# GpSimd builds every other second one-hot of the first tile, ScalarE the first ones of those quads

## The reference

```python
scores = einsum('thpc,hpnc->thpn', q, sub_keys)          # 8 heads, 2 halves, 128 keys
vals, idx = top_k(scores, 16)
top_vals, top_c = top_k(cand, 16)                        # of 16 x 16 sums per head
experts = (i1 * 128 + i2).reshape(T, 128)                # 128 of 16384 experts per token
gates = softmax(top_vals).reshape(T, 128)
# per block of 128 tokens:
u = take(expert_down, experts)                           # rows of 2048
hdn = gelu(einsum('ted,td->te', u, x))
y = einsum('te,ted->td', gates * hdn, take(expert_up, experts))
h = h + y;  return rms_norm(h, final_norm_gain)
```

## Time and profile before

| | |
|---|---|
| median of three runs | 2942.48 us |
| profiled execution | 2936.86 us |
| its span | 2935.1 us |
| PE busy | 2811.8 us (96%) |
| DVE busy | 2050.6 us (70%) |
| ACT busy | 1118.3 us (38%) |
| POOL busy | 542.0 us (18%) |
| row operations, down (L1976) | 256, 345.6 us, mean 1352 ns |
| gathers of down rows (L735) | 256, 261.6 us, mean 1022 ns |
| gathers of up rows (L735) | 256, 270.4 us, mean 1056 ns |

### The profile page before, as it was taken

How to read it: one execution, slowest core, us unless ns; L and a number is a source line. 1 busy time by engine, 2 the same in 40 slices (tenths; PEclk the granted TensorE clock), 3 DMA queues, 4 the chain that set the end, 5 groups by cost and what they waited for, 6 DMA issues and landing times.

```text
span 2935.1 us, 40591 instructions
## 1 busy us (share of the span) xinstructions
PE 2811.8 (96%) x15985; PEld 2275.7 (78%) x15985; DVE 2050.6 (70%) x3115; ACT 1118.3 (38%) x1743; POOL 542.0 (18%) x534
## 2 busy tenths in 40 slices
PE   6999999999999999899999999999999989999997
PEld 4788888887879988798897799888888877444443
DVE  4688877778765456744655669985559999666666
ACT  3344444445454445644455542112027986000000
POOL 1000000000000000000000002334435457544443
PEclk9999999999999999999999999999999999999999
DMA  9988888887866635365443646999998888999997
GB/s 362 361 288 271 270 269 269 270 268 269 294 201 179 174 112 167 124 201 170 136 130 122 202 135 231 351 339 409 407 356 284 295 295 322 408 409 409 409 409 319
DMA packets 345757, 799.55 MB, mean 272 GB/s; under 512 B 40104, under 2 KB 95648, under 8 KB 344800
## 3 DMA queue, kind: packets, MB, share of 16 engines
q1 hardware_dynamic: 270576, 505.70, 50.6%
q0 software_dynamic: 74992, 291.27, 26.4%
HBM read 794.76 MB, written 2.10 MB: 271 GB/s over the span
## 4 chain that ended last, share of the span: by engine, by line
PE 67%; DMA 14%; DVE 6%; ACT 5%; issue 4%; POOL 4%; SPq 0%; DVEq 0%; ACTq 0%; POOLq 0%
PE ps L2042 16%; PE ps L2044 15%; PE ps L2043 15%; PE ps L2607 13%; DMA s<-in_up_rows,s 12%; POOL s L735 3%; DVE s L1995 2%; DVE r L1268 1%; ACT s L1185 1%; DMA s<-in_down_rows,s 1%; DMA s<-in_ret_first 1%; DVE s L1976 1%; ACT s L1155 1%; ACT s L1163 1%; PE ps L2342 1%
## 5 line engine op out<-in xcount | busy, mean ns | idle before, releaser
L2042 PE MATMUL ps<-r,r 128*128 128x256 f32 (+1 forms) x2976 | 999.9, 336 | 14.8 <-DVE r L1268 12.4
L2044 PE MATMUL ps<-r,r 128*128 128x256 f32 (+1 forms) x2976 | 980.1, 329 | 0.0
L2043 PE MATMUL ps<-r,r 128*128 128x256 f32 (+1 forms) x2976 | 979.3, 329 | 0.0
L1268 DVE TENSOR_TENSOR r<-s,r 128x1024 fp32r<-128x1024 f32 (+2 forms) x532 | 640.1, 1212 | 418.9 <-ACT r L750 417.0
L750 ACT CAST r<-s 128x1024 fp32r<-128x1024 f32 (+2 forms) x532 | 549.0, 1039 | 740.2 <-PE ps L2044 696.8
L2042 PEld LDWEIGHTS ps<-r,r 128*128 128x128 f32 x2976 | 569.0, 191 | 81.0 <-issue 21.2
L2043 PEld LDWEIGHTS ps<-r,r 128*128 128x128 f32 x2976 | 569.3, 191 | 52.6 <-issue 5.3
L2044 PEld LDWEIGHTS ps<-r,r 128*128 128x128 f32 x2976 | 568.3, 191 | 50.5
L2732 PE MATMUL ps<-s,big 128*128 128x512 f32 x1024 | 441.6, 594 | 1.5 <-DMA s<-in_up_blocks 1.5
L1995 DVE SCALAR_TENSOR_TENSOR s<-s,s,s 128x1024 f32<-128x1024 f32 x256 | 328.8, 1284 | 162.3 <-DMA s<-in_up_rows,s 160.6
L1976 DVE CUSTOM_DVE_ANT_0 s<-s,s 128x1152 f32<-128x1152 f32 x256 | 345.6, 1352 | 97.3 <-DMA s<-in_down_rows,s 97.1
(11 more groups left out here) (315 smaller groups left out, 2244.1 us busy)
## 6 DMA issues: line engine op xcount, KB each, us to landing
s<-in_ada_w SPq DMA_DIRECT2D x128, 512.0 KB, 5.5
s<-in_up_blocks SPq DMA_DIRECT2D x128, 512.0 KB
s<-in_ret_w_in SPq DMA_DIRECT2D x112, 512.0 KB, 5.3
s<-in_down_blocks SPq DMA_DIRECT2D x128, 448.0 KB
s<-in_w_in SPq DMA_DIRECT2D x96, 512.0 KB, 3.9
s<-in_ret_w_out SPq DMA_DIRECT2D x64, 512.0 KB, 5.8
s<-in_ret_w_in SPq DMA_DIRECT2D x112, 256.0 KB, 4.1
s<-in_mla_w_in SPq DMA_DIRECT2D x48, 512.0 KB, 3.9
```

The costliest lines, as they stand in the source:

```text
L1268: v.tensor_tensor(lo_of(w), raw_of(w), hi_of(w).bitcast(F), ALU.subtract).then_inc(*lo_made.to(w))
L2042: pe.matmul(o, lh, rh, start=start, stop=False, skip_group_check=True)
L2043: pe.matmul(o, lh, rl, start=False, stop=False, skip_group_check=True)
L2044: return pe.matmul(o, ll, rh, start=False, stop=stop, skip_group_check=True)
```

## The change

`by_pool(t, q)` is true for the odd quads of tile 0. For them GpSimd makes the second ones, times the coefficients, into a buffer of its own, OHG, of four `tensor_scalar` instructions of 128x128: is LESS (minus i) equal to SECOND (minus i2), times CFT, the coefficient. ScalarE makes the first ones without coefficient, out of the PSUM bank: one Abs and one Relu of 128x512, into OH1[0]. VectorE has nothing to do in these quads. The even quads stay as they were.

```diff
+        OHG = at(W + 6144, 4, 128)
+        def by_pool(t, q):
+            return t == 0 and q % 2 == 1
...
+        ONES_AT = {min(195 + 2 * q, 255): q for q in range(1, 32, 2)}
...
+                if b == 129:
+                    sp.wait_ge(*built.at((0, 31)))
...
+            def pool_ones(q):
+                if q == 1:
+                    g.wait_ge(*block_used.at(127))
+                    g.wait_ge(*coef_copied.at(0))
+                else:
+                    g.wait_ge(*built.at((0, q - 2)))
+                for k in range(4):
+                    c = 4 * q + k
+                    r = g.tensor_scalar(OHG[:, k, :], LESS.bitcast(F), SECOND[0][:, c:c + 1], CFT[0][:, c:c + 1],
+                                        ALU.is_equal, ALU.mult)
+                r.then_inc(*pool_hot.to((0, q)))
...
+                if n in ONES_AT:
+                    pool_ones(ONES_AT[n])
...
-                    for k in range(4):
-                        c = 4 * q + k
-                        r = s.activation(o2[:, k, :], STEP, ACT.Abs, bias=SECOND[0][:, c:c + 1])
+                    if by_pool(0, q):
+                        o2 = OH1[0]
+                        s.wait_ge(*compared.at((0, q)))
+                        r = s.activation(flat(o2), bank[0], ACT.Abs)
+                    else:
+                        for k in range(4):
+                            c = 4 * q + k
+                            r = s.activation(o2[:, k, :], STEP, ACT.Abs, bias=SECOND[0][:, c:c + 1])
...
-                if n in HOT_AT:
+                if n in HOT_AT and not by_pool(0, HOT_AT.index(n)):
                     first_ones(0, HOT_AT.index(n))
...
-                free[b] = first_hot.at((t, q))
+                free[b] = (less_read if by_pool(t, q) else first_hot).at((t, q))
...
-                pe.wait_ge(*first_hot.at((t, q)))
+                pe.wait_ge(*(pool_hot if by_pool(t, q) else first_hot).at((t, q)))
                 pe.wait_ge(*second_hot.at((t, q)))
-                o1, o2 = (OH1[q % 2], OH2[q % 2]) if t else (OH1[0], OH2[0])
+                o1, o2 = (OH1[q % 2], OH2[q % 2]) if t else (OH1[0], OHG if by_pool(t, q) else OH2[0])
```

More of the change, by code:

```diff
@@ L496, in build @@
         d_x, d_pos, d_dec, d_fb = (dma_sig(n) for n in ("d_x", "d_pos", "d_dec", "d_fb"))
-        d_fg, d_tab, d_ff, d_f2, d_step = (dma_sig(n) for n in ("d_fg", "d_tab", "d_ff", "d_f2", "d_step"))
+        d_late, d_step = dma_sig("d_late", ["fg", "tab", "ff"]), dma_sig("d_step")
+        d_f2 = dma_sig("d_f2")
         d_out = dma_sig("d_out", range(2))
@@ L604, in build @@
         multiplied, picked = sig("multiplied", fours), sig("picked", fours)
-        first_hot = sig("first_hot", fours)
+        first_hot, pool_hot = sig("first_hot", [x for x in fours if not by_pool(*x)]), sig("pool_hot", [x for x in fours if by_pool(*x)])
         compared, less_read, second_hot = sig("compared", fours), sig("less_read", fours), sig("second_hot", fours)
@@ L716, in gpsimd @@
             g.wait_ge(*rotated.at(("M", 3)))
-            g.dma_start(GBA, A["final_norm_g"].partition_broadcast(128)).then_inc(*d_fg.to("all"))
+            g.dma_start(GBA, A["final_norm_g"].partition_broadcast(128)).then_inc(*d_late.to("fg"))
             g.wait_ge(*fin_scaled.at((3, 1)))
-            g.dma_start(GBA[:, 0:896], A["table"][:, K_DM:K_END]).then_inc(*d_tab.to("all"))
+            g.dma_start(GBA[:, 0:896], A["table"][:, K_DM:K_END]).then_inc(*d_late.to("tab"))
             g.wait_ge(*att_out.at(("L", 15)))
-            g.dma_start(FFG, A["ffn_norm_gain_2"][0][D1:].partition_broadcast(128)).then_inc(*d_ff.to("all"))
+            g.dma_start(FFG, A["ffn_norm_gain_2"][0][D1:].partition_broadcast(128)).then_inc(*d_late.to("ff"))
             g.dma_start(STEPN, A["table"][:, K_STEP:K_ALL]).then_inc(*d_step.to("all"))
+            def pool_ones(q):
[9 more added lines that the diff above has]
+                r.then_inc(*pool_hot.to((0, q)))
             g.wait_ge(*query_copied.at((3, 1)))
@@ L1375, in project_out @@
                             if n == 0:
-                                v.wait_ge(*d_fg.at("all"))
+                                v.wait_ge(*d_late.at("fg"))
                             v.tensor_tensor(XN[:, t, n * 512:(n + 1) * 512], X[:, t, n * 512:(n + 1) * 512],
@@ L1737, in vector @@
                 gate_side(i)
-            v.wait_ge(*d_tab.at("all"))
+            v.wait_ge(*d_late.at("tab"))
             def dil_groups():
@@ L1834, in vector @@
                 turn("E", p, colA[:, 64:80], None, HT)
-            v.wait_ge(*d_ff.at("all"))
+            v.wait_ge(*d_late.at("ff"))
             v.wait_ge(*turn_lo.at(("E", 7)))
```

## The result

| | before | after |
|---|---|---|
| median | 2942.49 us | 2995.20 us (2994.45 to 2997.14, 4 runs) |
| ratio | | 1.019, 95% interval 1.0172 to 1.0209 |
| profiled execution's span | 2935.1 us | 2992.7 us |
| last row operation of the down rows ends | 2408.8 us | 2464.5 us |

The kernel is slower by 53 us. The direction was forecast and the time lies in the range (2938 to 3000), but the loss is more than twice the +24 that was forecast. All but 2 us of it arises in the stretch that was named: the last down row is used 55.6 us later, and the spans of the two profiled executions differ by 57.6; behind that row 526.2 us followed before and 528.3 after.

The account below looks back on a forecast made before the run. ScalarE bounded the stretch at 8.08 us a pair of quads. Late gathers make it 9.6: +23 over 15 pairs, +2 at the start, -1.4 at the end, together +24, or 2966 us; range 2938 to 3000.

Parts of the forecast that it names:

- Where and who: Between 2280 and 2420 us VectorE waits for down rows, ScalarE falls to about 0.8 busy; stretch 20 to 30 us longer.
- the block: Block b = 129, held back until quad 31 is built, moves 512 KB later: 0, at most 1.3 us.
- A row operation holds GpSimd's SBUF-reading operations: A gather starting in a VectorE row operation begins only at its end; the new operations were expected to be held likewise.
- caught gathers: In odd quads two rows follow each other directly, so the gather between them is held, 0.8 us.
- One operation at 0.6 us: Assumed length of one new 128x128 GpSimd operation, between ScalarE's about 0.32 and a gather's 0.94.
- The group, 2.4 + 2.56 = 4.96 us: Four new GpSimd operations of 0.6 us plus two VectorE row operations of 1.28 running in between.
- The failed step: VectorE's pair of quads and the late gather's buffer loop settle at equal length, about 9.6 us against 8.08.
- the ring: Four row buffers: row n is gathered once row n-4 is used; loop 7.1 us, about 1.0 to spare.
- the gain: Rival: the ones fit GpSimd's idle half and no row is late; 2931 to 2936 us, chance 0.14.
- the draw: Rival: operations near 0.25 us, ScalarE's gain paid away in waits for rows; 2938 to 2947 us, chance 0.12.
- Much worse: Rival: each operation alternates with a row operation and takes over 1 us; pair 11.5 or more, 2990 to 3020, chance 0.14.
- gain if GpSimd were free: ScalarE's single Abs in odd quads saves 0.68 us; the pair takes 7.40, some 10 us over 15 pairs.

Follow-up runs that it names:

- e11: Changed kernel with five row buffers instead of four from row 196 on: 2991.78 us, ratio 1.0175.
- e2: Changed kernel without GpSimd's operations; TensorE multiplies odd quads with the second ones of the quad before (wrong result): 2939.27 us, ratio 1.0005.
- e6: Changed kernel with each GpSimd operation replaced by a memset of the same 128x128, reading nothing (wrong result): 2942.05 us, ratio 1.0011.
- e9: e2 plus a VectorE sum of 128x512, as long as the first ones, put back between the two adjacent rows: 2937.22 us, ratio 0.9991.
- e10: e2 with TensorE's compare of the next quad moved ahead of its build: 2940.36 us, ratio 1.0003.
- e13: Changed kernel with GpSimd's ones in every fourth quad only, waiting for the build of quad q-4 instead of q-2: 2964.31 us, ratio 1.0089.
- e3: Changed kernel with GpSimd's compare and multiply replaced by multiply twice (wrong one-hot): 2972.33 us, ratio 1.0111.
- e4: Changed kernel with one GpSimd operation ahead of each of four gathers, instead of all four ahead of one: 2997.58 us, ratio 1.0196.
- e7: Changed kernel with VectorE making the odd quads' second ones in four small operations, GpSimd none: 2947.63 us, ratio 1.0022.

## Why the prediction came out as it did

- *Where and who*: right. VectorE waits for in_down_rows, above all at the rows that were named, ScalarE falls from 0.98 busy to 0.57 (0.8 was said) and waits for TensorE, the tail keeps its length to 2 us, the block costs nothing. Not right was that one gather in four starts late: all of them do, which is the sign of a full list.
- *A row operation holds GpSimd's SBUF-reading operations*: right, for the new ones (41 of 64) and for caught gathers. The other direction, rows that wait for a new operation, which the prediction took from the Trainium skill ("SBUF — State Buffer"), came in three rows, for 0.06 to 0.25 us.
- *One operation at 0.6 us*: too low. It is 0.79 unheld. The bounds 0.10 to 0.94 held it.
- *The group, 2.4 + 2.56 = 4.96 us*: measured 90.6/16 = 5.66 on average.
- *The failed step* is the sentence "The two settle where they are equal: about 7.04 + (5.4 - 0.25)/2 = 9.6 us a pair". It shares the group's time between a late row and a late gather of a ring with four buffers. But GpSimd has four gathers to issue in each pair besides. Its own list by the prediction's own numbers is 4 x 0.94 + 3 x 0.31 + 0.16 + 4.96 + 0.4 = 10.2 us, longer than 9.6, and no halving applies to it. GpSimd, costed at 17.93 us of 40 before, was never added up as an engine after the change. e11 shows that the ring is not in it, the chain of waits (47% gathers, 49% ones) that the list is. It is not a matter of size alone: with the measured group of 5.66 the sentence would still give 7.04 + (5.66 + 0.4 - 0.25)/2 = 9.9 us, against the 11.9 that VectorE's rows show.
- *The sizes in the list*: with the measured ones it is 4 x 1.22 + 3 x 0.31 + 0.16 + 5.66 = 11.6; the whole list of 180.3 us over 16 groups is 11.3, since it has 59 gathers and not 64. So of the 2 us a pair between 9.6 and 11.6, 0.6 is the wrong bound, 0.7 the group and 0.7 the gathers held (18 of 59; 0.4 a pair was allowed for one, 1.1 came). With 10.2 the forecast would have been about +32; the rest is how often operations and gathers meet a row.
- *The rivals*: the gain and the draw are out (e2 and e6 are the draw: it needs an operation of 0.22 us that isn't held). "Much worse" has the right pair, 11.5, and the right time, 2990 to 3020, and its premise that an operation takes over 1 us was met with holds, 1.42. What it has wrong is that VectorE goes on doing four rows at 1.28: it waits for 4 to 5 us in each pair.
- *The prediction's "gain if GpSimd were free", 7.40 a pair*: wrong by itself, as e2, e9 and e10 show; ScalarE's new Abs waits for TensorE.

The Trainium skill ("GPSIMD Engine Reference", Performance versus the Vector engine) led to an estimate of up to 1.3 us an operation, or +53. The total came true, by luck: the operation itself was 0.79, and the holds made it 1.42. Nor does the prediction's own sum give +53 at 1.3 us: with its two row operations it is about +47, with three about +57.

## What to carry to other kernels

When work moves to an engine that looks half idle, add up that engine's whole list in the new order, with its instruction gaps and with the holds that the others inflict, before looking at buffers and waits: here 22 us free of 40 were not enough for four operations a pair, since 41 of the 64 met a row operation and 18 gathers did. An instruction in the queue of gathers delays everything behind it, and so does whatever it waits for (e13). And before a relief is counted as a gain, ask what the replaced instruction waited for and what the new one waits for.

## What the runs showed of the hardware

- An operation of GpSimd that reads SBUF and begins during a row operation of VectorE (two SBUF inputs) ends 0.66 to 0.67 us after that one's end (one of 0.58 apart); in e3, where it takes 0.44 us instead of 0.79, 0.32 us after (22 of 22). A memset isn't held (e6).
- The reverse hold exists, but is short: a row operation that starts less than 0.30 us behind the start of a free operation ends 1.65 us after that start, instead of 1.35 after its own (3 rows in after, 1.42 to 1.60 us long). One that starts 0.34 us or more behind takes its usual 1.36, though the operation goes on to 0.79. In e4, 14 rows that start 0.37 to 0.57 us behind a gather's start take 1.46 to 1.66 us. On the mean of all 256 rows, 1355 ns after against 1352 before, it doesn't show. The Trainium skill ("SBUF — State Buffer", SBUF: two separate sides) says that whichever started first has the shared port pair for the whole instruction and the other fully blocks. These records agree in both directions, except that VectorE waits only for the first 0.30 us of GpSimd's 0.79.
- Compare and multiply of 128x128 on GpSimd takes 0.79 us, multiply twice 0.44, a memset 0.22. The same compare and multiply on VectorE (e7) takes 1.04 us for four, start to start.
- The Trainium skill ("GPSIMD Engine Reference", Instruction dispatch) has about 6 us for the first call into freshly loaded code. Nothing of it was seen here, and whether the code was fresh isn't shown: the configuration records of 32 ns stand at 2275.7, and the first operation starts at 2276.56 and takes no longer than others.
- TensorE's granted clock, 1.00 in this stretch before, was 0.76 between 2290 and 2330 us after, part of the time at 2.4 and part at 1.2 GHz; its records fill 31.5 us of these 40, in part at the lower clock, where they filled 35.9 at full clock before. In e7, where VectorE hardly waits for rows (1.2 us in the stretch), the same 40 us are at 1.00 with 34.3. The chain of waits of after has no TensorE in it between 2290 and 2400 us, so the lower clock isn't what costs the time there; that the waits brought the clock down fits all runs here, but isn't shown by a run of its own.
